# A two-layer encoder trunk: order of score products, of loads and of additions changed at five places

## What is computed

```
# layer 0, 8 heads, two components of 64 features each
q, k = rms_norm(q, g) / 8, rms_norm(k, g)
logits = q @ k.T - slope * |t - s|          # for components 0 and 1, chunk-causal
wts = softmax(logits[0]) - lam * softmax(logits[1])
x = x + rms_norm(wts @ v) @ w_o
x = x + relu(rms_norm(x) @ w_up)**2 @ w_down
# k, v for layer 1, once; layer 1: 16 query heads, window of two chunks, a sink per head
x = x + attention(rms_norm(x) @ w_q, k, v, sinks) @ w_o
x = x + relu(rms_norm(x) @ w_up)**2 @ w_down
```

## Time and profile before

| | us |
|---|---|
| median of 3 runs | 2422.75 (2422.72 to 2424.11) |
| the profiled execution | 2419.25 |
| its span | 2417.5 |
| PE busy in the span | 2261.9 (94%) |
| PE weight loads busy | 1937.5 (80%) |
| DVE busy | 1602.9 (66%) |
| ACT busy | 1157.3 (48%) |
| POOL busy | 843.6 (35%) |

### The profile page before, as it was taken

One profiled execution on the slowest core, in us unless ns is written; L12 is line 12 of the kernel. 1 busy time (PEld: TensorE's weight loads), 2 busy tenths in 40 slices (PEclk: granted clock), 3 DMA queues, 4 the chain that ended last, 5 costly groups with the idle time before them and its releaser, 6 DMA issues.

```text
span 2417.5 us, 36501 instructions
## 1 busy us (share of the span) xinstructions
PE 2261.9 (94%) x11916; PEld 1937.5 (80%) x11916; DVE 1602.9 (66%) x3173; ACT 1157.3 (48%) x2476; POOL 843.6 (35%) x1461
## 2 busy tenths in 40 slices
PE   6999999987899999999999889998999999899998
PEld 5888888976678888777788888887778888688777
DVE  5577777776375666667766457875576666866773
ACT  4455555553355555534434246664455555533442
POOL 2333333335462222223335235553552222332331
PEclk9999999996999999999999899998999999999999
DMA  6001000000434444744552200002434444662452
GB/s 192 27 27 27 27 26 27 1 18 1 148 100 143 145 144 144 255 175 157 174 174 87 70 19 19 18 1 83 134 97 144 144 146 160 251 233 86 143 179 83
DMA packets 186756, 255.86 MB, mean 106 GB/s; under 512 B 15072, under 2 KB 135904, under 8 KB 181984
## 3 DMA queue, kind: packets, MB, share of 16 engines
q1 hardware_dynamic: 186592, 253.82, 31.5%
HBM read 174.09 MB, written 79.69 MB: 105 GB/s over the span
## 4 chain that ended last, share of the span: by engine, by line
PE 72%; DVE 15%; issue 6%; ACT 3%; DMA 2%; DVEq 1%; POOLq 1%; SPq 1%; POOL 0%; ACTq 0%
PE score L1738 40%; PE trb L1738 12%; PE proj L1738 11%; PE pv L1738 5%; DVE xop L1280 4%; DVE w_op L1280 2%; ACT p L951 1%; PE trb L2042 1%; DMA xop<-u_dram 1%; DVE p L1363 1%; DVE xT L1474 1%; PE trb L1776 1%; DVE p L1385 1%; DVE wa_lo L1280 1%; DVE pb L1685 0%
## 5 line engine op out<-in xcount | busy, mean ns | idle before, releaser
L1738 PE MATMUL score<-xop,w_op 128*128 128x512 f32 x3840 | 904.2, 395 | 29.1 <-DVE xT L1474 14.4
L1738 PEld LDWEIGHTS score<-xop,w_op 128*128 128x128 f32 x3840 | 727.7, 190 | 193.3 <-issue 41.1
L777 POOL TENSOR_TENSOR w_quad<-w_quad,w_sum 128x512 f32<-128x512 f32 x64 | 92.0, 1437 | 833.2 <-DVE w_op L1280 833.2
L1738 PE MATMUL trb<-xop,w_op 128*128 128x512 f32 x1536 | 360.4, 390 | 2.2 <-DVE quad L1474 1.6
L1738 PEld LDWEIGHTS trb<-xop,w_op 128*128 128x128 f32 x1536 | 287.7, 188 | 63.9 <-issue 4.2
L901 ACT ACTIVATE w_op<-w_quad 128x512 fp32r<-128x512 f32 (+1 forms) x336 | 216.6, 645 | 230.0 <-PE score L1738 166.3
L1280 DVE TENSOR_TENSOR w_op<-w_quad,w_op 128x512 fp32r<-128x512 f32 (+1 forms) x336 | 287.1, 858 | 49.9 <-ACT w_op L901 49.9
L1474 DVE TENSOR_TENSOR xT<-score,xT 128x512 f32<-128x512 f32 x160 | 109.8, 686 | 163.9 <-PE score L1738 155.4
L1738 PE MATMUL proj<-wa_hi,a_hi 128*128 128x384 f32 x480 | 166.9, 348 | 8.2 <-DVE wa_lo L1280 4.7
L1738 PE MATMUL score<-a_hi,w_op 128*128 128x512 f32 x512 | 161.3, 395 | 10.6 <-DVE w_op L1280 10.6
L951 ACT ACTIVATE p<-p,nm_a,slopes 128x256 f32<-128x256 f32 (+7 forms) x128 | 110.2, 862 | 112.1 <-DVE nm_a L1368 112.1
(11 more groups left out here) (252 smaller groups left out, 4583.3 us busy)
## 6 DMA issues: line engine op xcount, KB each, us to landing
xop<-u_dram SPq DMA_DIRECT2D x112, 512.0 KB, 6.6
u_dram<-quad SPq DMA_DIRECT2D x32, 1536.0 KB, 9.7
w_quad<-in_mlp_w_up SPq DMA_DIRECT2D x64, 512.0 KB, 5.7
w_quad<-in_mlp_w_down SPq DMA_DIRECT2D x64, 512.0 KB, 4.9
wa_raw<-in_a_w_qkv SPq DMA_DIRECT2D x96, 128.0 KB, 2.6
quad<-xT_dram SPq DMA_DIRECT2D x32, 256.0 KB, 3.8
xT_dram<-xs SPq DMA_DIRECT2D x32, 256.0 KB, 3.3
u_dram<-quad SPq DMA_DIRECT2D x32, 256.0 KB, 3.8
```

The lines of the kernel that those rows point to most:

```text
L777: return pool.tensor_tensor(out, x, y, ALU.subtract)
L1738: return nc.tensor.matmul(out, a, b, start=start, stop=stop, **kw)
```

## The change

On PE the scores go piece by piece, product by product, component by component; the wait on score_max covers both reads of the block before. SP asks for w_o panels 2 and 3 in segment 0 ahead of the wait on o_split. In the MLP, SP issues the raw parts of a slice ahead of the weight pair of the same place, and for pair NU + 1 = 17 the weight pair comes at place 5 instead of 3. DVE's loop takes the down pairs ahead of the up pairs of one place. PE spreads the row factors after product 7 instead of 5.

```diff
--- before.py
+++ after.py
@@ -562,6 +562,9 @@
                     sp.wait_ge(pb_ready, 6 * NB)
                 load_wo(0)
                 load_wo(1)
+                if seg == 0:
+                    load_wo(2)
+                    load_wo(3)
                 sp.wait_ge(o_split, KC * (seg + 1))
                 if seg:
                     sp.wait_ge(x_kept, 16 * 4)
@@ -569,7 +572,7 @@
                 load_pair(0)
                 load_unit(1)
                 for i in range(KC):
-                    if i + 2 < KC:
+                    if i + 2 < KC and (seg or i >= 2):
                         load_wo(i + 2)
                     if i in (3, 5):
                         u = (i + 1) // 2
@@ -616,12 +619,12 @@
 
                 for k in range(OPS + 6):
                     n, j = divmod(k, 7)
-                    if j == 3 and n + 2 < NP:
+                    for s, h in load_at(k):
+                        load_refill(s, h)
+                    if j == (5 if n == NU - 1 else 3) and n + 2 < NP:
 
                         sp.wait_ge(wop_split, products(seg, n, "S4"))
                         load_pair(n + 2)
-                    for s, h in load_at(k):
-                        load_refill(s, h)
                     if j == 5 and 1 <= n < NU:
                         store_rest(n - 1)
                     if j == 2 and 1 <= n < NU:
@@ -1586,7 +1589,7 @@
                     low(b_lo[:, c, cols], xT[:, c, cols], b_hi[:, c, cols]).then_inc(b_split, 1)
 
                 for k in range(OPS + 6):
-                    for n in range((k - 16) // 7, k // 7 + 1):
+                    for n in sorted(range((k - 16) // 7, k // 7 + 1), key=lambda n: (n < NU, n)):
                         at = k - 7 * n
                         if 0 <= n < NU:
                             if at in (4, 6, 8):
@@ -1809,16 +1812,17 @@
                     if attn:
                         if s % 2 == 0:
                             pe.wait_ge(kT_done, h * 4 + s // 2 + 1)
-                        for c in range(2):
-                            rows = slice(HD * c, HD * (c + 1))
-                            if not isinstance(h, int) or h or s:
-                                pe.wait_ge(score_max, t * 2 + c - 1)
-                            for k0 in range(0, P * (s + 1), HALF):
-                                k1 = min(k0 + HALF, P * (s + 1))
-                                q = slice(P * s, P * (s + 1))
-                                last = three(score[c][:, k0:k1], (qT_hi[rows, q], qT_lo[rows, q]),
-                                             (kT_hi[par][rows, k0:k1], kT_lo[par][rows, k0:k1]), True, True)
-                            last.then_inc(scores_ready, 1)
+                        if not isinstance(h, int) or h or s:
+                            pe.wait_ge(score_max, t * 2)
+                        q = slice(P * s, P * (s + 1))
+                        for k0 in range(0, P * (s + 1), HALF):
+                            k1 = min(k0 + HALF, P * (s + 1))
+                            for i, (qT, kT) in enumerate(((qT_hi, kT_hi), (qT_hi, kT_lo), (qT_lo, kT_hi))):
+                                for c in range(2):
+                                    rows = slice(HD * c, HD * (c + 1))
+                                    last = mm(score[c][:, k0:k1], qT[rows, q], kT[par][rows, k0:k1], i == 0, i == 2)
+                                    if i == 2 and k1 == P * (s + 1):
+                                        last.then_inc(scores_ready, 1)
                     lag = ("lag", s, 0) in uses
                     if lag:
                         transpose_weights(uses, s, (s - 1) % NB, t - 1)
@@ -1965,7 +1969,7 @@
                     last.then_inc(prod, 1)
                     if k == 3:
                         sum_squares()
-                    if k == 5:
+                    if k == 7:
                         spread_factors()
                     for n in range(NP - 4, NP - 1):
                         for t, when in enumerate((5, 7, 8, 9)):
```

## The result

The changed kernel took 2401.24 us (median of four executions, 2394.09 to 2407.31) against 2422.73 for the kernel before beside it (2421.76 to 2424.11): a ratio of 0.991 with a 95% interval of 0.9882 to 0.9938, 21.5 us less. The forecast was 2397 with a range of 2381 to 2411. Each kernel ran again for the experiments. Over all batches the kernel before took 2412.0 to 2425.9 in 50 executions (median 2420.0), the changed one 2394.1 to 2408.7 in ten (median 2401.5): 18.5 us less. The narrow spread of the first executions of before was chance; single executions of one kernel lie up to 14.6 us apart.

The account below looks back on a forecast made before the run. Heads: PE and DVE chains of nearly equal length; MLP: PE at full clock, broken by stalls. Terms 2.2 + 4.5 + 6.2 + 8.8 + 1.0 + 3.0 = 25.7 us off 2422.75 gave 2397 us, range 2381 to 2411.

Parts of the forecast that it names:

- Part 1: Heads: alternating score products brings component 1 forward 0.58 us in s = 4 to 7; 2.2 us taken, bounds 0 and 18.6.
- The term of 2.2 us: Heads 0 to 6: DVE's wait for PE's scores, in 6 cases, taken as the alternation's whole gain.
- PE idle rising by some 2 us a head: Heads: a sign; if PE's idle time did not rise by this much, the prediction would be wrong.
- (a): Rival, heads: PE bounds them after all, the whole 18.6 us of the alternation come through, 2381 us; 8%.
- (d): Rival, heads: alternation does nothing since PE chooses its order itself, 2399 us; 60% together with the forecast.
- Part 2: Projection by w_o: panels 2 and 3 loaded early, PE goes on at 625.1 instead of 629.59; 4.5 us gained.
- Part 3: MLP, row factors spread after product 7: wait after product 5 goes, 3.1 us a segment, 6.2 for two.
- The 0.35 us wait at product 7: MLP: PE's new wait there for up_add of S1, subtracted from the gain of 1.99 + 1.47 us a segment.
- Part 4: MLP turn: wait before product 121 goes, 8.8 us for two segments; wait at products 111 to 114 shrinks, 1.0 us.
- the delay of pair 17: MLP turn: the weight pair waits behind six transfers and lands about 2.7 us later, near 1016.2.
- The stall at product 115: MLP turn: a sign; a new stall there would make the prediction wrong, no size given.
- Part 5: MLP, three other slice starts: raw part's DVE operation begun first, 0.5 us for each of six, 3.0 us; bounds 0 and 7.

Follow-up runs that it names:

- (4, 5): The changed kernel with scores alternating only in row blocks s = 4 and 5 of a head: 2391.85 us, ratio 0.99.
- (6, 7): The changed kernel with scores alternating only in row blocks s = 6 and 7 of a head: 2397.82 us, ratio 0.991.

## Why the prediction held, and which steps of it didn't

- **Sum: high by 4 to 7 us, and the closeness of the two traces is luck.** 25.7 us forecast, 25.2 between the two traces, but 2.8 of these lie in layer 1, which the change doesn't touch. 22.4 are the change's in that pair, 21.5 in the first medians, 15.5 in the second, 18.5 in all executions. The parts run alone add up to 0 (alternation) + 9.6 + 12.8 = 22.4, but parts 2 to 5 together, in the kernel without the alternation, gave 16.7 (14 to 21); the intervals overlap. By the means of all profiled kernels the stages give 1.6 in the heads, 5.1 at the w_o wait, 5.5 at the factors, 6.9 in the turns and 0.4 at the slice starts: 19.5 us. What the forecast had too high is above all parts 4 (9.8) and 5 (3.0).
- **Part 1, right size for a wrong reason.** What the alternation does to PE came as told: both components start together, 0.58 us less a block. The term of 2.2 us was DVE's wait for scores in the earlier trace rows, and the step that failed is the one that read the whole gain of DVE's chain off that wait. Without a fall the (4, 5) kernels do heads 0 to 6 in 444.7 us, 6.0 below the mean of the old order. Set against the trace of before, DVE is idle 4.0 us less there (117.7 to 113.8) and busy 2.0 us less (333.0 to 331.0). Of the idle time 2.2 is that wait, which is gone, and 1.2 the wait before v_parts; why DVE is busy for less was not traced. And the prediction left the clock out of this part: it said where PE's surplus would go (PE idle rising by some 2 us a head; from 2.7 us in head 4 it rose by 1.2 to 1.5 in heads 4 to 6) but not that a wait of 0.7 us was being made one of 1.3, with a fall behind it. The two errors cancel: 1.6 us by the means of the traces, nothing in the medians. Of the rivals, (a) is refuted and (d) is what the medians show, though not by its mechanism.
- **Part 2, right.** The wait that is left is 3.83 us (9.06 less the forecast's 4.5 would be 4.56), ended by DVE's low part; that took 1.63 us, between the two rows, with POOL beside it for part of the time. In the nine kernels with the early loads this wait is 3.8 to 4.5 us, in the five others 8.3 to 9.5.
- **Part 3, right.** 3.1 us a segment in the two traces, 2.8 by the means. The 0.35 us wait at product 7 came as 0.5. I had worked it out from a trace with half clock at product 2; without that it is 2.0 us, which the prediction doesn't have. No stall came near product 11.
- **Part 4, right at product 121, wrong at product 114.** From the start of product 116 to that of 140 the kernel before takes 70.5 us, the changed one 66.0 in the trace shown, and so does the one with the additions alone: 4.5 us a segment for the 4.4 of the forecast. For products 112 to 115 the forecast had 0.5 us of gain. They took 18.5 us before, 19.6 and 18.1 in the changed kernel, and 19.0 in the mean of the twelve turns with both edits: 0.5 us lost, at the edge of its bounds. What it had too small was the delay of pair 17, 2.7 us: the pair landed 4.5 us later, and ACT stood 3.89 us for it. The stall at product 115, which the prediction names as a sign against itself, came (1.68 us), and 116 waits 1.15. That one need not accept this, by leaving pair 17 at place 3, the prediction did not see; then the same four products take 15.7 to 15.8 us, and a turn is 3 us shorter.
- **Part 5, wrong.** 3.0 us forecast, 0.2 a segment measured, and the kernel with SP's order alone has the same 0.2. The step was that a low part begun first would run beside no POOL sum. PE and DVE at the second slice (answers the earlier trace rows):

```profile
1101.37 3.92 PE L1741 MATMUL score<-xop,w_op 128*128 128x512 f32 x16 [1.08 <-DVE xop L1283]
```

```profile
1090.77 2.31 DVE L1283 TENSOR_TENSOR xop<-xop 128x1024 fp32r<-128x1024 f32 x1
```

The low part still takes 2.31 us, with POOL adding from 1090.38 to the end of it, and the wait of 1.07 us is where it was.

**A version that beats both.** The changed kernel with scores alternating in blocks 4 and 5 alone and pair 17 at place 3 takes 2389.5 us, ratio 0.9871: 30 us less than before beside it. The changed kernel was 15.5 and 21.5 us below before in its two batches.

## What to carry to other kernels

Where two engines' chains have nearly the same length, shorten the one only until it meets the other: what goes beyond that becomes a longer wait, and a longer wait of PE can cost more than the time that was saved. Look at the wait that your saving will end in, not only at the work that it removes. When single executions lie 14 us apart, read the gain stage by stage, and compare it with a stage that the edit can't have touched.

## What was not expected of the hardware

- The granted clock behind one and the same wait is 1.00 in one execution and 0.5 in another: behind a wait of 1.85 us product 2 takes 2.96 to 3.00 us in some segments and 4.2 to 4.6 in others. This makes part of the spread between executions, not shown to be all of it: in layer 1 the mean granted clock was 0.955 in the shortest of the 14 traces (416.8 us) and 0.932 in the longest (423.9), but traces with 0.931 lie between 418.9 and 422.7.
- The falls come in rows. In the three profiles of all-alternating heads and (6, 7) with three falls, these were in three neighbouring heads (1 to 3 twice, 3 to 5 once), and the heads beside them, with the same waits, had none.
- With the scores of blocks 6 and 7 alternating, the clock fell at the start of 21 of 30 heads (five kernels, heads 1 to 6); without, at 2 of 54 (nine kernels).
